# A two-layer decoder step on one core: norm parameters and p rows asked for during the last unit, the first weight half in two quarters

## The chip, the cores and the metric

The kernel runs on one core of one Trainium2 chip. The metric is the device time of one execution in microseconds (us). The engines are TensorE (PE, with PEld for its weight loads), VectorE (DVE), ScalarE (ACT), GpSimd (POOL) and SyncE (SP). SP issues most transfers through the hardware queue, GpSimd issues the others through the software queue, and all of them share 16 DMA engines.

## The reference

576 token rows of width 1024 (512 of a prompt, 64 of decode samples) pass through two layers. All arrays are float32.

```python
# layer 0: mixer A (chunked gMLP); layer 1: mixer B (short gated convolution)
x = layer_norm(DEEPNORM_ALPHA * x + mix, ln1_g[i], ln1_b[i])
moe = hier_moe(x, ...)      # 16 experts, two of them per token
x = layer_norm(DEEPNORM_ALPHA * x + moe, ln2_g[i], ln2_b[i])
gate = jax.nn.sigmoid(x @ ple_w_gate[i] + ple_b_gate[i])
x = x + gate * (p[i] @ ple_w_proj[i])
```

`layer_norm` is (x - mean) * rsqrt(var + 1e-5) * g + b over the 1024 columns. Mixer A begins with z = gelu(x @ w_in + b_in), whose second 3072 columns are v.

## The kernel before

Every float32 operand of a product is split into a high part `whi`, `xhi`, ... (ScalarE writes a rounded copy) and a low part `wlo`, `xlo`, ... (VectorE subtracts), and TensorE adds three products for one. A weight unit is 128x2048 numbers, 1 MB. SP loads it into one of the slots of `raw`, ScalarE's `hi` and VectorE's `lo` split it. Each engine's queue is written out by hand, in order, and the engines are joined by semaphores: where an instruction waits, all that follow it on its engine wait too.

**The start.** SP asks for row tile 0 of x, then for the first weight unit in two halves (semaphores `fh_ld` and `wld[0]`), then for four more row tiles and further units. TensorE turns row tile 0 (eight transposes), ScalarE writes the high part of the first half (L973) and then the two halves of `xhi` (L979), VectorE writes the low part of the first half (L1363) and then the two halves of `xlo` (L1371). TensorE's first product (L2106) needs all of these for its k. The first half holds the weights of k = 0 and 1; tile 1 of x is turned between k = 1 and k = 2.

**The end of mixer A.** The first 3072 columns are made in 12 units of seven products (Strassen's scheme; `q_done` counts products, QS = 7 per unit, US = 12 units). The products read `xhi`, `xlo` and the sums `xdh`, `xdl`. Products 0, 1 and 5 of a unit read `xhi`. After the last unit TensorE adds the last rows of the out projection, row tile by row tile (`out_rows`): for tiles 0 and 1 it turns the sum so far (L2268) and multiplies with `a_w_out` (L2277 to L2279). Then come `p_turns` (L2288, turns the rows of p), `h_turns(0)` (L2297, turns the normed rows of tile 0), and tile 2.

**The first norm of a layer.** VectorE takes the statistics of a row tile (L1602, L1604), ScalarE the root of the variance (L1104), VectorE subtracts the mean and multiplies with g (L1612), takes the reciprocal, and multiplies with it and adds b (L1617). g and b lie in the tile `ln_params` (`lnp`, 128x2048), in the place of `xhi`; the rows of p (`p_tok`) lie behind them in the place of `xhi` too. The result is alpha times the norm, for which GpSimd multiplies both g and b by alpha (L896). For layer 0, L1612 of row tile 0 also waits until the products of row tile 1 are done. GpSimd's queue at this place, in layer 0:

```python
pool.wait_ge(q_done, QS * US)              # L884: all products of the last unit
for n, g in enumerate((x_in["ln1_g"], x_in["ln1_b"])):
    pool.dma_start(lnp[:, n, :], ...)      # L887
pool.dma_start(p_tok[:, 0:4, :], ...)      # L888, and L889 for the sample rows
router_loads(0)                            # L859 to L862, four loads, layer 0 only
pool.wait_ge(ln_ld, 32 * (l + 1))
pool.tensor_scalar(lnp[:, :, :], lnp[:, :, :], ALPHA, None, ALU.mult).then_inc(ln_ok, 1)   # L896
```

In layer 1 the loads wait for the last products of the convolution's in projection instead (L885), and there are no router loads there. SP waits for all products of the last unit too (L640) and then reloads the other rows of the sum (`sum_reload`, L641), followed by expert weights (L668). VectorE's queue behind the norm of tiles 0 and 1 is: the split of the router weights (L1579 to L1582, layer 0), the low parts of p (L1636) and of the turned rows (L1640), the statistics of tile 2.

Behind the norm stand the router, a mixture of experts (16 steps, three weight units each), the second norm and the gate, and in layer 0 the convolution of layer 1.

Of the kernel before, what the change touches and what calls it, by code (L numbers as in the profile page):

```python
# [5 lines left out]
P = 128  # L6
# [79 lines left out]
def trunk(nc, x_in, outs):  # L86
# [60 lines left out]
    eps = new("eps", [P, 1])  # L147
# [174 lines left out]
    with ctx:  # L322
# [34 lines left out]
        xi_st, xb_ld = [sem("x_scaled_stored0"), sem("x_scaled_stored1")], sem("sum_reloaded")  # L357
# [228 lines left out]
        def _(sp):  # L586
# [24 lines left out]
            sp.dma_start(raw[:, 0, 0:UNIT // 2].rearrange("p (k c) -> p k c", c=512), first[:, 0:2, :]).then_inc(fh_ld, 16)  # L611
# [26 lines left out]
            def sum_reload():  # L638
                sp.wait_ge(xb_ld, 32)
                sp.wait_ge(q_done, QS * US)  # L640
                sp.dma_start(xcols(xT, PA, T), sum_dram[:, :, PA:T].rearrange("k p t -> p k t")).then_inc(xb_ld, 16)  # L641
# [118 lines left out]
        def _(pool):  # L760
# [15 lines left out]
            ch.link(pool.memset(eps[:, :], EPS))  # L776
# [102 lines left out]
            for l in range(DEPTH):  # L879

                if l == 0:
                    for n in range(4):
                        pool.wait_ge(acc_st[n], 32 * (AR - 1))
                    pool.wait_ge(q_done, QS * US)  # L884
                pool.wait_ge(mt_done, M_P[l] - KT)  # L885
                for n, g in enumerate((x_in["ln1_g"], x_in["ln1_b"])):
                    pool.dma_start(lnp[:, n, :], g[l:l + 1, :].to_broadcast([P, D])).then_inc(ln_ld, 16)  # L887
                pool.dma_start(p_tok[:, 0:4, :], x_in["p_prompt"][l, 0].rearrange("(i p) d -> p i d", p=P)).then_inc(p_ld, 16)  # L888
                pool.dma_start(p_tok[0:TS, 4, :], x_in["p_sample"][l].rearrange("b s d -> (b s) d")).then_inc(p_ld, 16)  # L889
                if l == 0:  # L890
                    router_loads(0)
# [4 lines left out]
                pool.tensor_scalar(lnp[:, :, :], lnp[:, :, :], ALPHA, None, ALU.mult).then_inc(ln_ok, 1)  # L896
# [66 lines left out]
        def _(act):  # L963
# [8 lines left out]
            act.wait_ge(fh_ld, 16)  # L972
            act.activation(whi[:, 0, 0:UNIT // 2], raw[:, 0, 0:UNIT // 2], ACT.Copy).then_inc(fh_ok, 1)  # L973
            for i in range(NT):
                act.wait_ge(tr_done, TR_IN + i + 1)
                for b in range(2):
                    src = ps[:, turned_bank(TR_IN + i) + b, :].rearrange("p (k t) -> p k t", t=P)[:, :, 0:tok(i)]
                    dst = xhi[:, 0:KT * T].rearrange("p (k t) -> p k t", t=T)[:, 4 * b:4 * b + 4, P * i:P * i + tok(i)]
                    act.activation(dst, src, ACT.Copy).then_inc(xhi_ok, 1)  # L979
# [120 lines left out]
            def std_tile(l, i):  # L1100

                t = tok(i)
                act.wait_ge(st_ok, NT * l + i + 1)
                act.activation(rstd[0:t, i:i + 1], mv[0:t, i, 1:2], ACT.Sqrt, bias=eps[0:t, 0:1]).then_inc(sq_ok, 1)  # L1104

            for l in range(DEPTH):
# [50 lines left out]
                act.activation(warm[:, :], eps[:, :], ACT.Exp)  # L1157
# [33 lines left out]
                def moe_step(s, it=0, step=0):  # L1191
# [4 lines left out]
                    if s == 0 and not step:  # L1196
                        act.activation(warm[:, :], eps[:, :], ACT.Silu)
# [87 lines left out]
                act.activation(warm[:, :], eps[:, :], ACT.Sqrt)  # L1285
# [67 lines left out]
        def _(dve):  # L1353
# [11 lines left out]
            half_lo(fh_ok, 0).then_inc(fh_ok, 1)  # L1365
            for i in range(NT):
                for b in range(2):
                    src = ps[:, turned_bank(TR_IN + i) + b, :].rearrange("p (k t) -> p k t", t=P)[:, :, 0:tok(i)]
# [224 lines left out]
            for l in range(DEPTH):  # L1593
# [12 lines left out]
                def norm_of(i):  # L1606
# [4 lines left out]
                    dve.wait_ge(ln_ok, l + 1)  # L1611
# [4 lines left out]
                    dve.wait_ge(rs_ok, 2 + n1 + i + 1)  # L1616
                    dve.scalar_tensor_tensor(out=xtok[0:t, i, :], in0=xtok[0:t, i, :], scalar=rstd[0:t, i:i + 1], in1=lnp[0:t, 1, :],  # L1617
# [425 lines left out]
        def _(pe):  # L2043
# [76 lines left out]
            for a in range(2):  # L2120
                for i in range(NT):
# [3 lines left out]
                    if i == 0 and a == 0:  # L2125
                        pe.wait_ge(fh_ok, 2)
                        v_half(0, a, i, range(0, 2))
# [129 lines left out]
            def out_rows(l, gl_n, d, pair_sem=None, pair_n=0):  # L2257
# [3 lines left out]
                def row_turns(i):  # L2261
                    if i >= 2:
                        pe.wait_ge(nz_ok, 2 * NT * l + i - 1)
                        if l == 0:
                            pe.wait_ge(xb_ld, 48)
# [104 lines left out]
                else:  # L2370
                    pe.wait_ge(xb_ld, 32)
# [363 lines left out]
```

## Time and profile before

| what | value |
|---|---|
| time, median of 3 runs | 1252.3 us (1251.42 to 1253.66) |
| profiled execution, its time | 1253.47 us |
| its span in the trace | 1251.4 us |
| TensorE busy | 1210.2 us, 97% |
| VectorE busy | 902.8 us, 72% |
| ScalarE busy | 618.6 us, 49% |
| GpSimd busy | 213.8 us, 17% |
| chain that ended last | TensorE 69%, DMA 13%, VectorE 9%, ScalarE 5%, issue 3%, GpSimd 1% |

The span runs from the first to the last instruction of the trace; the time of the same execution is 2.1 us longer. The chain that ended last is followed back from the last instruction, at each step to what released it. "Issue" is time in which an engine waited for nothing that the trace shows.

### The profile page before, as it was taken

What the parts mean: (1) busy time and instruction counts of PE and PEld (TensorE: products, weight loads), DVE (VectorE), ACT (ScalarE), POOL (GpSimd) and SP (SyncE); (2) the same over time, 40 slices, a digit from 0 to 9 for tenths busy, and PEclk for the clock granted to TensorE, in tenths of its full rate; (3) what the DMA queues carried; (4) which work ended last, traced back from release to release, by engine and by line L of the source; (5) the groups of instructions that cost most, each with busy time, mean ns of one, the idle gap of its engine ahead of it and who ended that gap; (6) DMA issues with size and microseconds to landing.
All of it is one profiled execution on the core that took longest, in us unless ns stands there. A gap on an engine that the chain in (4) does not pass through costs nothing.

```text
span 1251.4 us, 19263 instructions
## 1 busy us (share of the span) xinstructions
PE 1210.2 (97%) x7563; PEld 1094.5 (87%) x7563; DVE 902.8 (72%) x1238; ACT 618.6 (49%) x744; POOL 213.8 (17%) x246
## 2 busy tenths in 40 slices
PE   7999999999999998999999999999999999999898
PEld 6888889999999996888778699999998888878698
DVE  5554898687786876888889785445434889889793
ACT  5232444444344442488787574111211478878661
POOL 2311002131221312122431001000002022221100
PEclk9999999999999998999999999999999999999999
DMA  9456327594865954489998563322322369999522
GB/s 319 144 183 210 113 86 196 130 213 143 186 159 122 220 178 160 150 326 373 367 376 301 196 186 92 101 68 71 132 71 86 144 260 362 383 379 359 205 51 77
DMA packets 99583, 246.50 MB, mean 197 GB/s; under 512 B 10694, under 2 KB 55886, under 8 KB 87216
## 3 DMA queue, kind: packets, MB, share of 16 engines
q1 hardware_dynamic: 68976, 182.20, 41.4%
q0 software_dynamic: 30528, 63.20, 17.9%
q8 instruction: 55, 0.90, 0.3%
q14 instruction: 24, 0.20, 0.0%
HBM read 212.50 MB, written 49.62 MB: 209 GB/s over the span
## 4 chain that ended last, share of the span: by engine, by line
PE 69%; DMA 13%; DVE 9%; ACT 5%; issue 3%; POOL 1%; SPq 0%; DVEq 0%; POOLq 0%; ACTq 0%
PE ps L2055 13%; PE ps L2057 13%; PE ps L2056 13%; DMA w_raw<-in_moe_w_gate_up 7%; PE ps L2106 3%; PE ps L2108 3%; PE ps L2107 3%; PE ps L2471 2%; DVE w_lo L1359 2%; PE ps L2473 2%; PE ps L2472 2%; ACT w_hi L969 2%; DMA x_gathered<-y_scratch 1%; DMA ln_params<-in_ln_b 1%; PE ps L2163 1%
## 5 line engine op out<-in xcount | busy, mean ns | idle before, releaser
L1359 DVE TENSOR_TENSOR w_lo<-w_raw,w_hi 128x2048 fp32r<-128x2048 f32 (+1 forms) x133 | 290.2, 2191 | 66.6 <-ACT w_hi L969 58.0
L969 ACT ACTIVATE w_hi<-w_raw 128x2048 fp32r<-128x2048 f32 (+1 forms) x121 | 219.5, 1826 | 34.7 <-PE ps L2057 16.1
L2055 PE MATMUL ps<-x_hi,w_hi 128*128 128x288 f32 (+2 forms) x784 | 233.9, 298 | 1.9 <-DVE x_lo L1929 1.6
L2057 PE MATMUL ps<-x_hi,w_lo 128*128 128x288 f32 (+2 forms) x784 | 231.6, 295 | 0.0
L2056 PE MATMUL ps<-x_lo,w_hi 128*128 128x288 f32 (+2 forms) x784 | 231.6, 295 | 0.0
L2055 PEld LDWEIGHTS ps<-x_hi,w_hi 128*128 128x128 f32 x784 | 148.2, 189 | 3.6 <-issue 2.4
L2056 PEld LDWEIGHTS ps<-x_lo,w_hi 128*128 128x128 f32 x784 | 148.2, 189 | 0.0
L2057 PEld LDWEIGHTS ps<-x_hi,w_lo 128*128 128x128 f32 x784 | 148.2, 189 | 0.0
L2055 PE MATMUL ps<-g_hi,w_hi 128*128 128x288 f32 x384 | 114.6, 298 | 1.6 <-DVE g_lo L1495 0.7
L2057 PE MATMUL ps<-g_hi,w_lo 128*128 128x288 f32 x384 | 113.3, 295 | 0.0
L2056 PE MATMUL ps<-g_lo,w_hi 128*128 128x288 f32 x384 | 113.1, 294 | 0.0
L2471 PE MATMUL ps<-w_hi,xgT_hi 128*128 128x512 f32 x256 | 103.8, 406 | 6.3 <-DVE xgT_lo L1768 6.2
L2473 PE MATMUL ps<-w_hi,xgT_lo 128*128 128x512 f32 x256 | 100.9, 394 | 0.0
L2472 PE MATMUL ps<-w_lo,xgT_hi 128*128 128x512 f32 x256 | 100.2, 392 | 0.0
L1359 DVE TENSOR_TENSOR w_lo<-w_raw_more,w_hi 128x2048 fp32r<-128x2048 f32 x30 | 68.1, 2292 | 15.1 <-ACT w_hi L969 14.0
L2106 PE MATMUL ps<-w_hi,x_hi 128*128 128x512 f32 x192 | 75.8, 395 | 2.4 <-DVE x_lo L1371 2.4
L2055 PEld LDWEIGHTS ps<-g_hi,w_hi 128*128 128x128 f32 x384 | 72.1, 188 | 3.8 <-DVE g_lo L1495 1.6
L2108 PE MATMUL ps<-w_hi,x_lo 128*128 128x512 f32 x192 | 75.4, 392 | 0.0
L2107 PE MATMUL ps<-w_lo,x_hi 128*128 128x512 f32 x192 | 75.3, 392 | 0.0
L2056 PEld LDWEIGHTS ps<-g_lo,w_hi 128*128 128x128 f32 x384 | 72.1, 188 | 0.0
L2057 PEld LDWEIGHTS ps<-g_hi,w_lo 128*128 128x128 f32 x384 | 72.0, 188 | 0.0
L907 POOL DMA_INDIRECT x_gathered<-x_scratch,slot_token x32 | 41.2, 1288 | 152.7 <-PE ps L2437 123.6
(342 smaller groups left out, 2595.7 us busy)
## 6 DMA issues: line engine op xcount, KB each, us to landing
w_raw<-in_moe_w_gate_up SPq DMA_DIRECT2D x34, 1024.0 KB
w_raw<-in_moe_w_down SPq DMA_DIRECT2D x32, 1024.0 KB
w_raw_more<-in_moe_w_gate_up SPq DMA_DIRECT2D x30, 1024.0 KB
w_raw<-in_a_w_in SPq DMA_DIRECT2D x23, 1024.0 KB
w_raw<-in_a_w_out SPq DMA_DIRECT2D x12, 1024.0 KB
w_raw<-in_b_w_in SPq DMA_DIRECT2D x12, 1024.0 KB
sum_scratch<-out_stage POOLq DMA_DIRECT2D x40, 288.0 KB, 6.7
w_raw<-in_ple_w_gate SPq DMA_DIRECT2D x8, 1024.0 KB
```

The costliest lines, as they stand in the source:

```text
L907: pool.indirect_dma_start(out=xg[:, s % 2, :], out_offset=None, in_=x_dram[l][:, :], in_offset=bass.IndirectOffsetOnAxis(ap=idx[:, s:s + 1 ...
L969: act.activation(unit_of(whi, d), raw_unit(d), ACT.Copy).then_inc(hi_done, 1)
L1359: dve.tensor_tensor(unit_of(wlo, d), raw_unit(d), unit_of(whi, d).bitcast(f32), ALU.subtract).then_inc(split_done, 1)
L2055: pe.matmul(out, sh, mh, start=first, stop=False)
L2056: pe.matmul(out, sh, ml, start=False, stop=False)
L2057: ins = pe.matmul(out, sl, mh, start=False, stop=final)
L2106: pe.matmul(v_bank(i), xh_, wh, start=first, stop=False)
L2107: pe.matmul(v_bank(i), xh_, wl, start=False, stop=False)
L2108: ins = pe.matmul(v_bank(i), xl_, wh, start=False, stop=final)
L2471: pe.matmul(ps[:, 0, :], xs[0], ws[0], start=(a == 0 and k == 0), stop=False)
L2472: pe.matmul(ps[:, 0, :], xs[0], ws[1], start=False, stop=False)
L2473: ins = pe.matmul(ps[:, 0, :], xs[1], ws[0], start=False, stop=(a == 1 and k == 3))
```

## The change

The diff shows all edits but five in which `eps[:, :]` became `eps[:, 0:1]`.

```diff
     valid = new("valid", [P, NT])
-    eps = new("eps", [P, 1])
+    eps = new("eps", [P, 2])
     cols = new("cols", [P, NCOL])
...
         td_ok, tdh_ok, tdl_ok = sem("x_combined"), sem("x_combined_hi_ready"), sem("x_combined_lo_ready")
-        xi_st, xb_ld = [sem("x_scaled_stored0"), sem("x_scaled_stored1")], sem("sum_reloaded")
+        xi_st, xb_ld = [sem("x_scaled_stored0"), sem("x_scaled_stored1")], sem("part_loaded")
         acc_st = [sem(f"sum_added{n}") for n in range(4)]
...
             first = rows4(w_in, 0, AW)
-            sp.dma_start(raw[:, 0, 0:UNIT // 2].rearrange("p (k c) -> p k c", c=512), first[:, 0:2, :]).then_inc(fh_ld, 16)
+            for n, quarter_ld in enumerate((fh_ld, xb_ld)):
+                sp.dma_start(raw[:, 0, 512 * n:512 * n + 512], first[:, n, :]).then_inc(quarter_ld, 16)
             sp.dma_start(raw[:, 0, UNIT // 2:].rearrange("p (k c) -> p k c", c=512), first[:, 2:4, :]).then_inc(wld[0], 16)
...
             def sum_reload():
-                sp.wait_ge(xb_ld, 32)
+                sp.wait_ge(xb_ld, 48)
                 sp.wait_ge(q_done, QS * US)
...
             pool.memset(valid[:, :], 1.0)
-            ch.link(pool.memset(eps[:, :], EPS))
+            pool.memset(eps[:, 0:1], EPS)
+            ch.link(pool.memset(eps[:, 1:2], EPS / ALPHA ** 2))
             ch.link(pool.memset(wss[:, :, :], 0.0))
...
                         pool.wait_ge(acc_st[n], 32 * (AR - 1))
-                    pool.wait_ge(q_done, QS * US)
+                    pool.wait_ge(q_done, QS * (US - 1) + 1)
                 pool.wait_ge(mt_done, M_P[l] - KT)
...
                     pool.dma_start(lnp[:, n, :], g[l:l + 1, :].to_broadcast([P, D])).then_inc(ln_ld, 16)
+                if l == 0:
+                    pool.wait_ge(q_done, QS * US - 1)
                 pool.dma_start(p_tok[:, 0:4, :], x_in["p_prompt"][l, 0].rearrange("(i p) d -> p i d", p=P)).then_inc(p_ld, 16)
...
                 if l == 0:
+                    pool.wait_ge(q_done, QS * US)
                     router_loads(0)
...
                 pool.wait_ge(ln_ld, 32 * (l + 1))
-                pool.tensor_scalar(lnp[:, :, :], lnp[:, :, :], ALPHA, None, ALU.mult).then_inc(ln_ok, 1)
+                pool.tensor_scalar(lnp[:, 1, :], lnp[:, 1, :], ALPHA, None, ALU.mult).then_inc(ln_ok, 1)
                 for i in range(NT):
...
 
-            act.wait_ge(fh_ld, 16)
-            act.activation(whi[:, 0, 0:UNIT // 2], raw[:, 0, 0:UNIT // 2], ACT.Copy).then_inc(fh_ok, 1)
+            def quarter_hi(n):
+                act.wait_ge((fh_ld, xb_ld)[n], 16)
+                if n:
+                    act.wait_ge(fh_ok, 2)
+                act.activation(whi[:, 0, 512 * n:512 * n + 512], raw[:, 0, 512 * n:512 * n + 512], ACT.Copy).then_inc(fh_ok, 1)
+
+            quarter_hi(0)
             for i in range(NT):
...
                 for b in range(2):
+                    if i == 0 and b:
+                        quarter_hi(1)
                     src = ps[:, turned_bank(TR_IN + i) + b, :].rearrange("p (k t) -> p k t", t=P)[:, :, 0:tok(i)]
...
                 act.wait_ge(st_ok, NT * l + i + 1)
-                act.activation(rstd[0:t, i:i + 1], mv[0:t, i, 1:2], ACT.Sqrt, bias=eps[0:t, 0:1]).then_inc(sq_ok, 1)
+                act.activation(rstd[0:t, i:i + 1], mv[0:t, i, 1:2], ACT.Sqrt, bias=eps[0:t, 1:2], scale=1 / ALPHA ** 2).then_inc(sq_ok, 1)
 
...
 
-            half_lo(fh_ok, 0).then_inc(fh_ok, 1)
+            def quarter_lo(n):
+                dve.wait_ge(fh_ok, 1 + 2 * n)
+                c = slice(512 * n, 512 * n + 512)
+                dve.tensor_tensor(wlo[:, 0, c], raw[:, 0, c], whi[:, 0, c].bitcast(f32), ALU.subtract).then_inc(fh_ok, 1)
+
+            quarter_lo(0)
             for i in range(NT):
                 for b in range(2):
+                    if i == 0 and b:
+                        quarter_lo(1)
                     src = ps[:, turned_bank(TR_IN + i) + b, :].rearrange("p (k t) -> p k t", t=P)[:, :, 0:tok(i)]
...
                         dve.wait_ge(mt_done, rows_done(0, 1))
-                    dve.wait_ge(ln_ok, l + 1)
+                    dve.wait_ge(ln_ld, 32 * (l + 1))
                     dve.scalar_tensor_tensor(out=xtok[0:t, i, :], in0=ps[0:t, b:b + 2, :].rearrange("p b t -> p (b t)"), scalar=mv[0:t, i, 0:1],
...
                     dve.wait_ge(rs_ok, 2 + n1 + i + 1)
+                    dve.wait_ge(ln_ok, l + 1)
                     dve.scalar_tensor_tensor(out=xtok[0:t, i, :], in0=xtok[0:t, i, :], scalar=rstd[0:t, i:i + 1], in1=lnp[0:t, 1, :],
...
                     if i == 0 and a == 0:
-                        pe.wait_ge(fh_ok, 2)
-                        v_half(0, a, i, range(0, 2))
+                        for n in range(2):
+                            pe.wait_ge(fh_ok, 2 + 2 * n)
+                            v_half(0, a, i, range(n, n + 1))
                         input_turn(1)
...
                         if l == 0:
-                            pe.wait_ge(xb_ld, 48)
+                            pe.wait_ge(xb_ld, 64)
                     for k in range(KT):
...
                 else:
-                    pe.wait_ge(xb_ld, 32)
+                    pe.wait_ge(xb_ld, 48)
                     pe.wait_ge(c_done, CS * US - 2)
...
                     pe.wait_ge(c_done, CS * US)

```

The edits, in words:

- Start: the first half of the first weight unit is asked for as two transfers of 128x512 (`fh_ld` and `xb_ld`, so later waits on `xb_ld` count 16 more). ScalarE and VectorE split each quarter by itself; the second quarter's split stands between the two halves of tile 0 of x on both engines. TensorE waits for one quarter before k = 0 and for the other before k = 1.
- Layer 0: GpSimd asks for g and b once the first product of the last unit is done, for the rows of p once its sixth is done, for the router's arrays once all seven are done.
- Both layers: GpSimd multiplies only b by alpha. g stays as loaded: ScalarE takes the root of (var + eps) / alpha^2 instead, at the same place. VectorE's first pass waits for the loads, its second pass for GpSimd.

## Rows read from the trace of the kernel before

**Rows 1.** The chain that ended last, in order of time: start us, length us, what.
```profile
7.19 1.23 DVE w_lo L1363
...
461.57 11.30 DMA ln_params<-in_ln_b
...
472.96 5.40 POOL ln_params L896
...
478.48 1.28 DVE x_tok L1612
...
587.38 15.50 DMA w_raw<-in_moe_w_gate_up
...
946.69 5.97 DMA ln_params<-in_ln_b
...
952.75 5.40 POOL ln_params L896
```

**Rows 2.** Timeline of the start, all engines: start us, length us, engine line operation.
```profile
4.77 1.94 PE L2048 MATMUL ps<-ident,x_rows_in 128*128 128x128 f32 x8 [4.77 <-DMA x_rows_in<-in_x_prompt]
...
6.10 1.06 ACT L973 ACTIVATE w_hi<-w_raw 128x1024 fp32r<-128x1024 f32 x1 [4.01 <-DMA w_raw<-in_a_w_in]
...
7.06 1.06 ACT L979 ACTIVATE x_hi<-ps 128x512 fp32r<-128x512 f32 x2
...
8.33 1.28 DVE L1371 TENSOR_TENSOR x_lo<-ps,x_hi 128x512 fp32r<-128x512 f32 x2
...
9.07 0.80 PE L2106 MATMUL ps<-w_hi,x_hi 128*128 128x512 f32 x1 [2.36 <-DVE x_lo L1371]
```

**Rows 3.** Timeline of TensorE where layer 0's first norm begins.
```profile
473.94 0.40 PE L2279 MATMUL ps<-w_hi,g_lo 128*128 128x512 f32 x1
...
477.88 1.97 PE L2288 MATMUL ps<-ident,p_tok 128*128 128x128 f32 x8 [3.55 <-DMA p_tok<-in_p_sample]
...
481.56 1.97 PE L2297 MATMUL ps<-ident,x_tok 128*128 128x128 f32 x8 [1.71 <-DVE x_tok L1617]
```

**Rows 4.** Timeline of TensorE where layer 1's first norm begins.
```profile
958.34 1.03 PE L2288 MATMUL ps<-ident,p_tok 128*128 128x128 f32 x8
...
960.97 1.09 PE L2297 MATMUL ps<-ident,x_tok 128*128 128x128 f32 x8 [1.60 <-DVE x_tok L1617]
```

**Rows 5.** Timeline of VectorE, layer 0's first norm.
```profile
466.00 3.49 DVE L1359 TENSOR_TENSOR w_lo<-w_raw,w_hi 128x2048 fp32r<-128x2048 f32 x3
...
485.66 0.22 DVE L1579 MEMSET w_router_hi_lo<- 128x192 f32 x1
...
491.62 1.29 DVE L1602 BATCH_NORM_STATS2 v_stats<-ps 128x6 f32<-128x512 f32 x2 [2.89 <-PE ps L2279]
```

**Rows 6.** Timeline of VectorE, layer 1's first norm.
```profile
953.47 0.21 DVE L1604 BATCH_NORM_AGGREGATE mean_var<-v_stats 128x2 f32<-128x12 f32 x1
...
968.56 1.29 DVE L1602 BATCH_NORM_STATS2 v_stats<-ps 128x6 f32<-128x512 f32 x2 [1.16 <-PE ps L2279]
```

**Rows 7.** Stretches with TensorE's busy time: granted clock, share of DMA, GB/s.
```profile
449.00:460.00 11.00, 11.00 (x86) 1.00 0.01 1
...
477.00:486.50 9.50, 6.90 (x28) 0.50 0.38 148
...
958.40:962.80 4.40, 2.80 (x26) 1.00 0.10 41
```

**Rows 8.** Timeline of the issuing queues and of ScalarE around the last unit.
```profile
452.45 0.41 ACT L1061 ACTIVATE g_full<-ps 128x288 f32<-128x288 f32 x1 [0.95 <-DVE g_lo L1495]
...
460.39 0.36 SPq L641 DMA_DIRECT2D xT<-sum_scratch  x1
...
465.74 0.56 POOL L862 DMA_DIRECT2D b_router<-in_moe_b_expert  x1
...
509.88 0.33 SPq L668 DMA_DIRECT2D w_raw_more<-in_moe_w_gate_up  x1
```

**Rows 9.** Transfers of 440 to 480 us: size, microseconds from issue to landing.
```profile
b_router<-in_moe_b_expert POOLq DMA_DIRECT2D x1, 8.0 KB, 15.0
```

More of the change, by code:

```diff
@@ L1156, in _ @@
                 std_tile(l, 4)
-                act.activation(warm[:, :], eps[:, :], ACT.Exp)
+                act.activation(warm[:, :], eps[:, 0:1], ACT.Exp)
                 proj_out(1)
@@ L1196, in moe_step @@
                     if s == 0 and not step:
-                        act.activation(warm[:, :], eps[:, :], ACT.Silu)
+                        act.activation(warm[:, :], eps[:, 0:1], ACT.Silu)
                     q = it * step + (NE * l + s)
@@ L1283, in out_copy @@
                     act.activation(o_sb[0:tok(i), i, 512 * h:512 * h + 512], out_bank(u)[0:tok(i), :], ACT.Copy).then_inc(out_a, 1)
-                act.activation(warm[:, :], eps[:, :], ACT.Sqrt)
+                act.activation(warm[:, :], eps[:, 0:1], ACT.Sqrt)
                 squares(0)
```

## The prediction

> **What bounds the kernel now.** I read the page first: TensorE is busy for 97% of the span, and 69% of the chain that ended last is its work, so a change counts only where that chain leaves TensorE. Then I read the chain in order of time and looked for other engines' pieces. Three places belong to this change [rows 1]: the split of the first weight half at 7.19; in layer 0 a load of the norm's parameters of 11.30 us, followed by GpSimd's product of 5.40; in layer 1 the same pair with 5.97 and 5.40. The timelines of those places say what each waits for, the stretches say at which clock TensorE ran there, and the queues and landings say what the moved loads will meet. In layer 0 TensorE ends its products at 474.34 (473.94 + 0.40), idles 3.55 us for the rows of p, turns them, and idles 1.71 more for the first normed tile [rows 3]. In layer 1 it idles only 1.60, because its products last until 958.34 and the turns of p follow at once [rows 4].
>
> **The start.** Before, VectorE splits the whole first half (7.19 + 1.23 = 8.42) and only then takes x [rows 1, 2]: its first half of x is done near 8.97, and TensorE's first product comes 0.1 later, at 9.07. ScalarE began that half of x at 7.06 though the turned rows were there at 6.71 (4.77 + 1.94), since its weight copy ended only then [rows 2]. After: the half weight landed at 6.07, 1.3 us behind x; its first quarter has half the bytes and should land near 5.4. Its copy takes about 0.6 (a little over half of 1.06) and its subtraction about 0.68, so both end by 6.75. ScalarE takes x at 6.75 to 7.35, VectorE to 8.02 (halves of the pairs of 1.06 and 1.28), and the first product starts near 8.12: 0.95 earlier. The second quarter is copied by 7.95 and subtracted by 8.70; TensorE needs it after three products, which it begins 0.43 apart at this point, so after 9.4. The second weight half is split by about 10.8 and needed near 11.9. The extra issue delays the later x tiles by some 0.4 us on SP, which the two products' time covers. What can eat into 0.95 is the slow pace of the first products: if the pace doubles at the same moment as before and not with the work, half of the 0.95 is lost. Bounds 0.5 and 1.0; I take 0.8, nearer to the top, because each step has a row. From here to 452 the chain holds TensorE and its splits, so this is carried along.
>
> **Layer 0, loads.** The first product of the last unit is done by 452.45, when ScalarE takes it; all seven are done by 460.39, when SP's reload goes out [rows 8]. Between 449 and 460 the DMA engines are 1% busy [rows 7]. So g and b, asked for at 452.5 and 453.1, should land as in layer 1, 5.97 us behind the second issue [rows 1], or near 459; even with the 11.30 of before they are there by 465. The condition for the rows of p falls one product before the end, about (460.39 - 452.45) / 6 = 1.3 earlier, at 459.1, and their second issue at 459.9. Before, they landed at 477.88 with 1 MB of parameters ahead of them, some 15 us behind their issue. If they still took 15 us they would be there at 474.9, and their turns (1.03 at full clock [rows 4]) would be over at 476, before the normed tile. I expect them near 470, under the products. The router's last load was issued at 465.74 and landed 15.0 later, at 480.7 [rows 8, 9]; VectorE takes it at 485.66 [rows 5]. Four issues are gone from ahead of it (some 2.3 us), so with the same delay it lands at 478.4, and VectorE will ask at 481.6: hidden by 3. GpSimd waits at this place with nothing behind it but these issues and the scaling.
>
> **Layer 0, the norm.** GpSimd's product has half the elements: 2.7 us of the 5.40 [rows 1]. It runs behind the router's issues, near 464 to 466.7, long before VectorE's second pass. VectorE's first pass then waits only for the products of row tile 1, which end at 474.34. Before, TensorE's turns came 3.08 us behind the start of that pass (481.56 - 478.48) [rows 1, 3]. So they start at 474.43 + 3.08 = 477.5 and not at 481.56: **4.05 us**. The turns of p lie in the gap before.
>
> **Layer 0, the clock.** From 477.0 to 486.5 TensorE ran at a granted clock of 0.50, its lower level of 1.2 GHz, after it had idled 3.55 us [rows 7, 3]. In layer 1 the same turns, with an idle time of 1.60 between them, ran at 1.00, the 2.4 GHz level [rows 7, 4]. From the turns of tile 0 to the statistics of tile 2 layer 0 takes 491.62 - 481.56 = 10.06 and layer 1 takes 968.56 - 960.97 = 7.59 [rows 3 to 6]. Afterwards TensorE idles in layer 0 from about 475.4 to 477.5, 2.1 us, which is nearer to the 1.60 than to the 3.55. I take it that the clock holds: **2.45 us** more. VectorE has time for this: it idles 1.16 in layer 1 before those statistics [rows 6], and the split of the router weights, four short operations from 485.66 on, is the only work that layer 0 has beyond that [rows 5]. Together 6.5 us. The Trainium skill, "TensorE: Matmul & The Clock Gate", section on PE-mode transpose, says that turns don't engage the full clock as products do. By that rule the clock would fall here, for nothing but turns runs from 474.3 to 479.3, and the sum would be 6.45 in place of 8.9. The trace speaks against it in layer 1, where 4.4 us of turns and idle time kept 1.00 [rows 7].
>
> **Layer 1.** The loads are not moved. They land at 952.75 [rows 1]; VectorE has its statistics at 953.68 [rows 6] and can start its first pass there, while GpSimd scales b until 955.45. The second pass ends near 956.8, before 958.34 + 1.03 = 959.37, when the turns of p are through. The wait ends there and TensorE is the bound: 960.97 - 959.37 = **1.60 us** [rows 4]. A slower scaling would still be hidden by 2.5 us. ScalarE's root with a scale is the same instruction; the second memset is a tenth of a microsecond on GpSimd, at the start, before anyone asks for it.
>
> **What carries it to the end.** The next expert loads are issued at 509.88, when the row products are through [rows 8], so they move with the chain, and so does the stream of weights whose 15.50 us the chain contains at 587.38 [rows 1].
>
> **The sum.** 0.8 + 6.5 + 1.6 = 8.9 us off the profiled execution's 1253.5 (span 1251.4 and 2.1 around it): 1244.6. The median of the runs is 1.2 below that execution, so I forecast 1252.3 - 8.9 = 1243.4 us.
>
> **The rivals.**
> - *The clock falls all the same in layer 0* and the stretch takes its 10.06 us: the gain is 0.8 + 4.05 + 1.6 = 6.45, time 1245.9. For it: 2.1 us of idle time with only turns on both sides has no row. Against it: layer 1 with 1.60. Chance 0.20.
> - *GpSimd's scaling collides with VectorE.* Before, it stood beside statistics; now it stands at 464 to 466.7, beside a low part of g and the first of the three `w_lo` at 466.00 [rows 5], which read two arrays in SBUF. That `w_lo` ends near 468.3 and TensorE needs it 0.3 later. If the two engines took turns for the 1.4 us of overlap, TensorE would lose 1.1: time 1244.5. No row shows such an overlap. The Trainium skill, "GPSIMD Engine Reference", section on specifications, says that the two contend when VectorE has two SBUF inputs. Chance 0.10.
> - *The stream of expert weights absorbs it.* If the stretch around 587 were bound by transfers whose pace is not tied to the row stage, all before it would be lost and 1.6 remain: 1250.7. Against it: the issue at 509.88. Chance 0.05.
> - *The loads don't come earlier where it matters*: the rows of p wait behind the reload of x and the expert weights until 477.9 as before. The turns of p then run at the lower clock to 479.85, the gain in layer 0 is 1.7, and the time 1252.3 - 4.1 = 1248.2; where g and b are late too, there is no gain in layer 0 and it is 1249.9. Chance 0.07.
> - *Slower: the clock falls at 475.4 and stays down.* Before, it was down for some 10 us. Each microsecond of work at 1.2 GHz costs half of one. With the 8.9 gained, the time passes that of before once 18 us are spent there; if it lasted until the router is through at 530, it would cost 25 and give 1268. Nothing in the profile shows so long a fall. Chance 0.03.
>
> **How the numbers follow.** The forecast keeps 0.55. Its own range is 1242.3 to 1244.7: the terms at 9.1 and 8.6 and about 1 us between runs. The stated range, 1241.5 to 1247.0, takes in the first two rivals and leaves out 0.15. A measurement of this kernel can tell about 0.2%, 2.5 us, from no change. Below 1249.8 lie the forecast, the first two rivals and the first part of the fourth: 0.90. Within 0.2%: the stream, and the late g and b, 0.07. Slower: 0.03.
>
> **What would show it.** First product near 8.1. `ln_params` issued at about 452 and landed by 459, L896 2.7 us long before 467. TensorE goes from its products into the turns of p without waiting, idles about 2 us, turns tile 0 about 3.1 us behind the products' end, at a clock of 1.00, and the statistics of tile 2 follow 7.6 later. In layer 1 no idle time before L2297. The prediction is wrong if the clock row reads 0.50 there, if `w_lo` at 466 is longer than 2.3, or if a new DMA wait stands on TensorE before 530.

## The result and the profile after

| what | before | after |
|---|---|---|
| time, median of 6 runs each on one chip | 1252.05 us (1251.01 to 1253.66) | 1245.21 us (1242.97 to 1247.69) |
| profiled execution, its time | 1253.47 us | 1246.35 us |
| its span | 1251.4 us | 1243.9 us |
| ratio after / before, 95% interval | | 0.9944 [0.9929, 0.9959] |

The change makes the kernel 6.8 us faster, where 8.9 were forecast; the time lies within the stated range. The six executions of the changed kernel fall into two groups of three: 1242.97, 1243.89 and 1244.08, which is near the forecast 1243.4, and 1246.35, 1246.41 and 1247.69. The median, 1245.21, lies between the groups, where no execution was. TensorE's mean granted clock is on record for each execution: 1.000 for all three of the first group, 0.999, 0.998 and 0.999 for the second. The profiled execution (0.999) belongs to the second group, so its trace can say what is missing. One execution of an experiment below (e1) took 3053.67 us and is left out of its ratio.

**The start.** Timeline of all engines in the changed kernel, which answers [rows 2] (L1380 splits a quarter, L2126 to L2128 are the products, L2068 turns x):

```profile
5.89 0.69 DVE L1380 TENSOR_TENSOR w_lo<-w_raw,w_hi 128x512 fp32r<-128x512 f32 x1 [5.89 <-ACT w_hi L981]
6.69 0.60 ACT L991 ACTIVATE x_hi<-ps 128x512 fp32r<-128x512 f32 x1 [0.82 <-PE ps L2068]
...
8.06 0.79 PE L2126 MATMUL ps<-w_hi,x_hi 128*128 128x512 f32 x1 [1.41 <-DVE x_lo L1390]
...
10.79 1.91 PE L2068 MATMUL ps<-ident,x_rows_in 128*128 128x128 f32 x8
...
12.92 0.63 PE L2127 MATMUL ps<-w_lo,x_hi 128*128 128x512 f32 x1
...
13.35 0.55 PE L2128 MATMUL ps<-w_hi,x_lo 128*128 128x512 f32 x1
...
13.74 0.40 PE L2126 MATMUL ps<-w_hi,x_hi 128*128 128x512 f32 x1
```

The same stretch of TensorE before the change:

```profile
11.79 1.32 PE L2048 MATMUL ps<-ident,x_rows_in 128*128 128x128 f32 x8
12.87 0.47 PE L2106 MATMUL ps<-w_hi,x_hi 128*128 128x512 f32 x1
...
13.64 0.40 PE L2106 MATMUL ps<-w_hi,x_hi 128*128 128x512 f32 x1
```

The first product starts at 8.06, 1.01 us earlier than at 9.07 [rows 2], each step as forecast. But products that take 0.63 us (slow pace) turn into products that take 0.40 (full pace) at 13.4 to 13.7 in the changed kernel; before, the pace had doubled by 12.9. The eight turns between k = 1 and k = 2 take 1.91 us where they took 1.32. At the first product of k = 3 (13.74 against 13.64) nothing is left of the 1.01 in this pair of traces. The granted clock is shown as 1.00 in these stretches in both kernels. But the record behind that column has its first entry only at 13.7 us in the changed kernel's trace and at 12.4 in the one before (an estimate, counted back from the falls near 477), which is where the pace doubles; the slow pace ahead of it is seen in the durations alone.

**Layer 0.** TensorE in the changed kernel, the answer to [rows 3] (L2309 turns p, L2318 the normed tile 0, L2289 the sum of tile 2):

```profile
474.52 0.39 PE L2300 MATMUL ps<-w_hi,g_lo 128*128 128x512 f32 x1
474.75 1.03 PE L2309 MATMUL ps<-ident,p_tok 128*128 128x128 f32 x8
477.73 1.87 PE L2318 MATMUL ps<-ident,x_tok 128*128 128x128 f32 x8 [1.95 <-DVE x_tok L1637]
479.39 1.91 PE L2289 MATMUL ps<-ident,xT 128*128 128x128 f32 x8
```

VectorE and GpSimd there, the answer to [rows 5] and [rows 8]:

```profile
465.90 0.76 DVE L1514 TENSOR_TENSOR g_lo<-g_full,g_hi 128x576 fp32r<-128x576 f32 x1 [0.76 <-ACT g_hi L1060]
466.58 3.49 DVE L1371 TENSOR_TENSOR w_lo<-w_raw,w_hi 128x2048 fp32r<-128x2048 f32 x3
...
475.00 1.28 DVE L1631 SCALAR_TENSOR_TENSOR x_tok<-ps,mean_var,ln_params 128x1024 f32<-128x1024 f32 x1 [1.24 <-PE ps L2300]
...
476.39 1.28 DVE L1637 SCALAR_TENSOR_TENSOR x_tok<-x_tok,rstd,ln_params 128x1024 f32<-128x1024 f32 x1
...
486.98 1.29 DVE L1621 BATCH_NORM_STATS2 v_stats<-ps 128x6 f32<-128x512 f32 x2 [2.08 <-PE ps L2300]
```

```profile
451.48 0.54 POOL L889 DMA_DIRECT2D ln_params<-in_ln_b  x1
459.60 0.76 POOL L892 DMA_DIRECT2D p_tok<-in_p_prompt  x1 [7.58 <-PE ps L2077]
...
464.49 2.83 POOL L901 TENSOR_SCALAR ln_params<-ln_params 128x1024 f32<-128x1024 f32 x1
```

The stretches, the answer to [rows 7] (us, TensorE busy, granted clock, share of DMA, GB/s):

```profile
474.90:477.70 2.80, 0.88 (x9) 1.00 0.47 196
478.00:481.00 3.00, 3.00 (x17) 0.50 0.43 172
482.00:486.50 4.50, 4.50 (x21) 1.00 0.28 117
```

VectorE's first pass waits for the products alone (1.24 us, released by TensorE), and the turns of p follow the products at once. From the end of the products to the turns of tile 0 it is 477.73 - 474.91 = 2.82 us, where it was 481.56 - 474.34 = 7.22 [rows 3]: 4.40 gained. At 478 the granted clock falls to 0.50, the 1.2 GHz level, and is back at 1.00 (2.4 GHz) by 482. From the turns of tile 0 to the statistics of tile 2 it takes 486.98 - 477.73 = 9.25 us, against 10.06 before and 7.59 in layer 1: 0.81 of the forecast 2.45 is gained.

**Layer 1.** TensorE in the changed kernel, the answer to [rows 4], and VectorE, the answer to [rows 6]:

```profile
953.35 1.03 PE L2309 MATMUL ps<-ident,p_tok 128*128 128x128 f32 x8
954.22 1.04 PE L2318 MATMUL ps<-ident,x_tok 128*128 128x128 f32 x8
```

```profile
950.58 1.28 DVE L1637 SCALAR_TENSOR_TENSOR x_tok<-x_tok,rstd,ln_params 128x1024 f32<-128x1024 f32 x1 [0.49 <-POOL ln_params L901]
...
961.75 1.30 DVE L1621 BATCH_NORM_STATS2 v_stats<-ps 128x6 f32<-128x512 f32 x2 [1.62 <-PE ps L2300]
```

No idle time is left. From the turns of p to the statistics of tile 2 it takes 8.40 us where it took 968.56 - 958.34 = 10.22: 1.82 gained.

So the two traces differ by 4.40 + 0.81 + 1.82 = 7.0 us in the norms. The times of the two executions differ by 7.1 and their spans by 7.5; what differs elsewhere nearly cancels. At the end of layer 0's products the changed kernel's trace is 0.57 us behind (474.91 against 474.34), 0.1 of it from the start and some 0.4 from a late piece of ScalarE and VectorE near 294 us. Before, TensorE had another slow stretch in layer 1's experts, which the changed kernel's trace hasn't; it is worth about 1.7 us (an estimate: half of the 3.4 us that it lasted, since at 0.53 the same work takes about twice the time):

```profile
1107.90:1111.50 3.60, 3.60 (x11) 0.53 0.83 330
```

Most of that was lost again: from the statistics of tile 2 in layer 1 to TensorE's last turns (which start at 1235.82 before and at 1228.81 after) the lead grows by 0.2 us only. Why wasn't followed.

### The profile page after: what moved, and what is told of

Its sections match the earlier page's. It is cut to its first block, busy times and chain, and to the rows that moved or that the text cites. A ratio compares the mean times of both kernels' runs of the same rounds, so it can differ in the third digit from the quotient of the medians.

```text
span 1243.9 us, 19268 instructions
## 1 busy us (share of the span) xinstructions
PE 1208.4 (97%) x7563; PEld 1093.4 (88%) x7563; DVE 903.1 (73%) x1239; ACT 618.2 (50%) x745; POOL 210.1 (17%) x247
## 4 chain that ended last, share of the span: by engine, by line
PE 72%; DMA 12%; DVE 9%; ACT 4%; issue 3%; SPq 0%; DVEq 0%; POOLq 0%; ACTq 0%
PE ps L2075 13%; PE ps L2077 13%; PE ps L2076 13%; DMA w_raw<-in_moe_w_gate_up 8%; PE ps L2126 3%; PE ps L2127 3%; PE ps L2128 3%; DVE w_lo L1371 2%; PE ps L2492 2%; PE ps L2494 2%; PE ps L2493 2%; ACT w_hi L974 2%; PE ps L2298 2%; PE ps L2300 1%; PE ps L2299 1%
## 5 line engine op out<-in xcount | busy, mean ns | idle before, releaser
L2126 PE MATMUL ps<-w_hi,x_hi 128*128 128x512 f32 x192 | 76.1, 396 | 1.4 <-DVE x_lo L1390 1.4
L2128 PE MATMUL ps<-w_hi,x_lo 128*128 128x512 f32 x192 | 75.5, 393 | 0.0
```

The source lines that it names most:

```text
L2126: pe.matmul(v_bank(i), xh_, wh, start=first, stop=False)
L2128: ins = pe.matmul(v_bank(i), xl_, wh, start=False, stop=final)
```

## The experiments

The times below are medians and ratios to the kernel before, on the same chip in the same set of executions.

### Which part carries the gain: e1 and e2

e1 is the kernel before with the start's edits alone, e2 the changed kernel without them.

```diff
-            sp.dma_start(raw[:, 0, 0:UNIT // 2].rearrange("p (k c) -> p k c", c=512), first[:, 0:2, :]).then_inc(fh_ld, 16)
+            for n, quarter_ld in enumerate((fh_ld, xb_ld)):
+                sp.dma_start(raw[:, 0, 512 * n:512 * n + 512], first[:, n, :]).then_inc(quarter_ld, 16)
```

> Only the start of the change: the first weight half in two quarters; the norm as before. Theory A (the first product comes 1.0 us earlier, but TensorE reaches its full pace at a moment that isn't tied to it): first product at 8.1 against 9.07, and at 40 us anything between 1.0 earlier and level; median time 0 to 1 us under the kernel before. Rival (the gain is carried whole, what was lost in the changed kernel came from the norm's part): 1.0 us under. Rival (the extra transfer delays the later tiles of x): a new wait for x rows before 25 us, time over that of before.

> Only the norm's part of the change; the first weight half as before. Theory A: 6 to 8.5 us under the kernel before, within 1 us of the changed kernel, since the start gives little. Rival (the start gives its 1.0): 1.0 us over the changed kernel. In both, executions lie in two groups some 2 to 3 us apart, by whether TensorE's clock falls behind the gap in layer 0.

Measured: e1 1252.03 us, ratio 0.9994 [0.9984, 1.0003]; e2 1246.45, ratio 0.9945 [0.9932, 0.9959]. The start's part is worth 0.8 us by its ratio, with no gain at all inside its interval, and the rest alone gives the changed kernel's ratio (0.9944). Everything that is clear of the noise comes from the norm's part. In e1's trace the first product starts at 8.02 and TensorE is at full pace by 12.3; in the changed kernel's it was 13.7. How much of the 1 us survives differs from execution to execution, so one pair of traces can't price it. All traces together can, roughly. The first product of k = 3 starts at 13.48 to 14.67, on average 13.90, in the six traces with the first half in one piece (before, e2, e3, e4, e7, e8), and at 12.72 to 13.74, on average 13.06, in the four with quarters and no extra turns at the start (the changed kernel, e1, e5, e6): 0.84 us earlier. At the split of a weight unit near 455 us, the same averages are 455.72 and 455.24, 0.48 us apart, with ranges that overlap.

### The loads and the scaling, each alone: e3 and e4

e3 is the kernel before with the early loads alone (g and b both scaled, as before). e4 is the kernel before with the halved scaling alone (the loads at their old time).

```diff
 e3
-                    pool.wait_ge(q_done, QS * US)
+                    pool.wait_ge(q_done, QS * (US - 1) + 1)
...
+                if l == 0:
+                    pool.wait_ge(q_done, QS * US - 1)
                 pool.dma_start(p_tok[:, 0:4, :], ...)
...
                 if l == 0:
+                    pool.wait_ge(q_done, QS * US)
                     router_loads(0)
 e4
-                pool.tensor_scalar(lnp[:, :, :], lnp[:, :, :], ALPHA, None, ALU.mult).then_inc(ln_ok, 1)
+                pool.tensor_scalar(lnp[:, 1, :], lnp[:, 1, :], ALPHA, None, ALU.mult).then_inc(ln_ok, 1)
...
-                    dve.wait_ge(ln_ok, l + 1)
+                    dve.wait_ge(ln_ld, 32 * (l + 1))
...
+                    dve.wait_ge(ln_ok, l + 1)
```

> Only the earlier loads of layer 0; g and b are both scaled by GpSimd as before. Theory (in layer 0 the loads are what counts, since the scaling of 5.4 us now lies under the products; in layer 1 the scaling is what counts): layer 0 as in the changed kernel, turns of tile 0 about 2.9 us behind the end of the products; layer 1 unchanged, with TensorE idle 1.6 us; 1.7 us over the norm-only kernel, about 4.5 to 6.5 under the kernel before. Rival (GpSimd's scaling beside VectorE's splits costs): the low part of the weights at 466 takes over 2.3 us and TensorE waits for it.

> Only the scaling of b alone, with the loads asked for when they were before. Theory: in layer 0 the rows of p now end the wait: they land near 477.9 as before, their turns follow, and the turns of tile 0 directly behind them at 479.9, 1.7 us earlier than before, at the lower clock; layer 1 gains 1.7; 3.4 us under the kernel before. Rival (the parameters end the wait, p is by the way): layer 0 gains 4, as in the changed kernel.

Measured: e3 1250.01 us, ratio 0.9983 [0.9974, 0.9992]; e4 1245.87, ratio 0.9956 [0.9942, 0.9969]. Both expectations failed. e3 brings 2.1 us where 4.5 to 6.5 were expected, and its rival came true in part: not the low part of the weights but one of g is longer, and TensorE waits for it (next section). For e4, 3.4 us were expected, and half the scaling alone brings 5.5 us of the changed kernel's 7.0 by the ratios; the two intervals overlap. (Each ratio's distance from 1, times 1252.)

Timeline of e4, GpSimd, VectorE and TensorE:

```profile
462.85 0.57 POOL L890 DMA_DIRECT2D p_tok<-in_p_sample  x1
...
472.15 2.79 POOL L897 TENSOR_SCALAR ln_params<-ln_params 128x1024 f32<-128x1024 f32 x1 [5.84 <-DMA ln_params<-in_ln_b]
```

```profile
474.44 1.28 DVE L1613 SCALAR_TENSOR_TENSOR x_tok<-ps,mean_var,ln_params 128x1024 f32<-128x1024 f32 x1 [1.25 <-PE ps L2281]
...
476.17 1.28 DVE L1619 SCALAR_TENSOR_TENSOR x_tok<-x_tok,rstd,ln_params 128x1024 f32<-128x1024 f32 x1 [0.37 <-DVE rstd L1616]
```

```profile
476.93 1.09 PE L2290 MATMUL ps<-ident,p_tok 128*128 128x128 f32 x8 [2.58 <-DMA p_tok<-in_p_sample]
477.86 1.04 PE L2299 MATMUL ps<-ident,x_tok 128*128 128x128 f32 x8
```

With the loads at their old time, g and b have landed by 472.1, 2.3 us before the products end. What had kept VectorE's first pass until 478.48 [rows 1] was the scaling of g behind the landing, not the landing. Now that pass reads g as loaded and waits for the products alone (1.25 us), and GpSimd scales b before the second pass asks for it. The rows of p land at 476.9. Their turns then fill the time in which VectorE finishes tile 0, and the turns of tile 0 follow without a wait at 477.86, 3.5 us behind the products, against 2.82 in the changed kernel. In this trace the clock held, so the statistics of tile 2 come 7.54 us behind those turns (485.40 - 477.86), against 9.25.

### GpSimd and VectorE side by side: e3, e7, e8

e7 is e3 with the scaling in two instructions of 128x1024. e8 is e3 with the scaling held back until ScalarE and VectorE have split the last part of g.

```diff
 e7
-                pool.tensor_scalar(lnp[:, :, :], lnp[:, :, :], ALPHA, None, ALU.mult).then_inc(ln_ok, 1)
+                pool.tensor_scalar(lnp[:, 0, :], lnp[:, 0, :], ALPHA, None, ALU.mult)
+                pool.tensor_scalar(lnp[:, 1, :], lnp[:, 1, :], ALPHA, None, ALU.mult).then_inc(ln_ok, 1)
 e8
+                if l == 0:
+                    pool.wait_ge(gl_done, ROUND * AR)
                 pool.tensor_scalar(lnp[:, :, :], lnp[:, :, :], ALPHA, None, ALU.mult).then_inc(ln_ok, 1)
```

> The loads-only kernel (loads of layer 0 early, g and b both scaled), with GpSimd's scaling of 128x2048 written as two instructions of 128x1024. In the loads-only kernel one low part of g on VectorE took 2.90 us in place of 0.76 while GpSimd scaled. If the long single instruction is what holds VectorE up: 0.76 again, 2 us under the loads-only kernel (1248). If it is any work of GpSimd at this moment: as the loads-only kernel, 1250.

> The loads-only kernel, with GpSimd's scaling of 128x2048 held back until VectorE's last low part of g is done (near 466); it then stands beside the three low parts of weights. If GpSimd and VectorE get in each other's way whenever VectorE reads two arrays in SBUF: one of the low parts of weights is longer by up to 2 us, TensorE waits, 1250 or more. If not: every low part as long as before, 1248.

Measured: e7 1249.63 us, ratio 0.9977 [0.9968, 0.9987]; e8 1248.01, ratio 0.9962 [0.9950, 0.9973]. Timelines of GpSimd and VectorE, first e3, then e7, then e8:

```profile
463.86 5.43 POOL L899 TENSOR_SCALAR ln_params<-ln_params 128x2048 f32<-128x2048 f32 x1
...
465.27 2.90 DVE L1498 TENSOR_TENSOR g_lo<-g_full,g_hi 128x576 fp32r<-128x576 f32 x1 [0.75 <-ACT g_hi L1051]
468.10 3.48 DVE L1362 TENSOR_TENSOR w_lo<-w_raw,w_hi 128x2048 fp32r<-128x2048 f32 x3
```

```profile
464.04 2.83 POOL L899 TENSOR_SCALAR ln_params<-ln_params 128x1024 f32<-128x1024 f32 x1
466.82 2.78 POOL L900 TENSOR_SCALAR ln_params<-ln_params 128x1024 f32<-128x1024 f32 x1
...
465.46 0.76 DVE L1499 TENSOR_TENSOR g_lo<-g_full,g_hi 128x576 fp32r<-128x576 f32 x1 [0.76 <-ACT g_hi L1052]
466.13 5.10 DVE L1363 TENSOR_TENSOR w_lo<-w_raw,w_hi 128x2048 fp32r<-128x2048 f32 x3
```

```profile
467.41 7.26 POOL L901 TENSOR_SCALAR ln_params<-ln_params 128x2048 f32<-128x2048 f32 x1 [2.38 <-DVE g_lo L1500]
...
467.14 6.94 DVE L1364 TENSOR_TENSOR w_lo<-w_raw,w_hi 128x2048 fp32r<-128x2048 f32 x3
```

e7's first half of the scaling leaves `g_lo` at 0.76, but the time is that of the second case, any work of GpSimd. In e8 the low parts are longer, as in its first case, but the time is that of the second, 1248. The 5.40 us scaling beside VectorE's subtractions costs time, in another place each time: in e3 one `g_lo` takes 2.90 us in place of 0.76, in e7 the three `w_lo` take 5.10 in place of 3.49 [rows 5], in e8 they take 6.94 and the scaling itself 7.26. TensorE feels it most in e3, where `g_lo` is awaited:

```profile
468.23 0.50 PE L2280 MATMUL ps<-w_hi,g_hi 128*128 128x512 f32 x1 [0.92 <-DVE g_lo L1498]
```

In the changed kernel the scaling of b alone, beside the same `g_lo` and the first 0.7 us of `w_lo`, costs nothing: 0.76 and 3.49, as before. So halving it does two things: it ends the wait, and it makes the early place harmless. Why 2.83 us of GpSimd's work there isn't felt and 5.4 us is, in two instructions as in one, stays open.

e8 shows something else too. It scales g and b in full and gains nothing in layer 1 (TensorE idles 1.39 us there), yet its ratio is worth 4.8 us, where e3's is worth 2.1. So the early loads can end layer 0's wait without the halving, if the scaling stays clear of the `g_lo` that TensorE waits for. In its trace the turns of tile 0 start 3.2 us behind the products (478.65 - 475.47), where it was 7.22. The two edits are two ways to about the same gain in layer 0.

### The clock in layer 0's gap: e5 and e6

Both are the changed kernel with work for TensorE between the turns of p and those of tile 0 in layer 0, in banks that nothing reads before they are written again. The results aren't used.

```diff
                 p_turns(0)
                 p_turns(1)
+                if l == 0:
+                    gap_work(n)
                 h_turns(0)
 e5: 8 products of 128x512 of constants, some 2.1 us
 e6: 17 turns of 128x128 of constants, some 2.0 us
```

> The changed kernel, with eight extra products of ones (128x512, result unused) on TensorE in layer 0's gap between the turns of p and the turns of tile 0, where it idles 1.95 us. Theory B (the gap is what makes the clock fall in some executions): the clock stays at the 2.4 GHz level, 7.6 us from the turns of tile 0 to the statistics of tile 2 in place of 9.25, the time is near 1243 in all executions, about 2 us under the changed kernel's median. Rival (the clock falls for another reason, or not there in most executions): no change in median or spread.

> The changed kernel, with 17 extra turns (transposes of a tile of ones, result unused) in the same gap in place of products. If turns hold the clock as products do: as with the products, near 1243 in all executions. If turns don't count for it: a stretch of 5 us of nothing but turns, the clock falls in most executions, and the time is 1246 or more.

Measured: e5 1244.46 us (1243.03 to 1246.21), ratio 0.9935 [0.9921, 0.9949]; e6 1243.43 (1242.62 to 1244.56), ratio 0.9922 [0.9909, 0.9936]. Timeline of TensorE and stretches in e6:

```profile
473.96 1.03 PE L2309 MATMUL ps<-ident,p_tok 128*128 128x128 f32 x8
474.83 2.02 PE L2376 MATMUL ps<-ident,ones 128*128 128x128 f32 x17
...
476.94 1.09 PE L2318 MATMUL ps<-ident,x_tok 128*128 128x128 f32 x8
```

```profile
474.80:478.90 4.10, 4.00 (x36) 1.00 0.31 124
```

From 474.0 to 478.9 TensorE does nothing but turns, and the clock stays at 1.00. The statistics of tile 2 stand at 484.53, 7.59 behind the turns of tile 0: the forecast's number. By the ratios (0.9935 and 0.9922 against 0.9944, times 1252) work in the gap brings 1.1 and 2.8 us; the intervals overlap with the changed kernel's, so neither is clear of the noise by itself. e6 shows no execution above 1244.6, e5 has two, 1245.40 and 1246.21, so "near 1243 in all executions" failed for e5. The three executions of e5 with a mean granted clock of 1.000 (1243.03, 1243.91, 1244.46) and the three of e6 (1242.62, 1243.43, 1244.56) are as fast as the three of the changed kernel with 1.000. That the gap's idle time makes the clock fall is therefore likely, since both traces with work in it held the clock there, but not proved: e9's and e4's traces hold it too without such work, and falls come elsewhere as well (e6's trace has one near 1130 us, in layer 1's experts). The Trainium skill, "TensorE: Matmul & The Clock Gate", section on PE-mode transpose, has it that transposes don't engage the full clock; by the row above, and by e9 below, it doesn't hold here. A fall such as it would give did come in the changed kernel's profiled execution, but not from the turns: with more of them in the gap the clock held.

### The start: e9 and e10

e9 is the changed kernel with 13 turns of constants before x has landed and 6 behind the turns of tile 0; e10 adds e6's turns in the gap. None of their results is used.

```diff
+            pe.wait_ge(ident_ok, 1)
+            start_turns(13)
             pe.wait_ge(ident_ok, 2)
...
             input_turn(0)
+            start_turns(6)
```

> The changed kernel, with 13 extra turns of a tile of ones on TensorE before x arrives and 6 more behind the turns of row tile 0 (results unused). Theory A (TensorE's pace doubles after it has worked for a while, and turns count as work): the pace doubles before 10 us in place of 13.7, the products of the start run at 0.23 us apart earlier, 2 to 3 us under the changed kernel. Rival (turns don't count): the doubling stays at 12 to 14 us, same time.

> The changed kernel with both fillings of turns, at the start and in layer 0's gap: the sum of both, near 1241, and the least spread between executions.

Measured: e9 1243.34 us, ratio 0.9927 [0.9914, 0.9940]; e10 1241.81 (1241.12 to 1243.77), ratio 0.9915 [0.9902, 0.9928]. e9 is 2.1 us under the changed kernel by the ratios, as theory A has it, but the intervals overlap; e10 is 3.6 us under it, and its interval lies just below the changed kernel's. Timeline of TensorE in e9:

```profile
1.74 2.98 PE L2098 MATMUL ps<-ident,ones 128*128 128x128 f32 x13 [1.74 <-POOL ident L766]
4.68 1.07 PE L2068 MATMUL ps<-ident,x_rows_in 128*128 128x128 f32 x8
5.58 0.82 PE L2098 MATMUL ps<-ident,ones 128*128 128x128 f32 x6
7.22 0.50 PE L2133 MATMUL ps<-w_hi,x_hi 128*128 128x512 f32 x1 [0.81 <-DVE x_lo L1390]
...
7.79 0.40 PE L2135 MATMUL ps<-w_hi,x_lo 128*128 128x512 f32 x1
9.20 0.50 PE L2133 MATMUL ps<-w_hi,x_hi 128*128 128x512 f32 x1 [1.02 <-DVE w_lo L1380]
```

The turns of constants alone bring TensorE to full pace: those of x take 1.07 us where they took 1.94, and the first products take 0.40, not 0.63. (In e12's trace it comes later: the turns of x still take 1.91 us, the first products 0.40.) With that the earlier work is kept: TensorE has the third product of k = 2 at 12.00, where the changed kernel has it at 13.35. A new wait of 1.02 us stands before k = 1, for the second quarter's low part, which the slow pace had hidden. The clock in the gap stayed at 1.00 in e9's trace without any filling.

### The early loads with the clock held: e11 and e12

e12 is e10's kernel once more. e11 is the same with the loads at their old time, and with the 17 turns ahead of those of p.

```diff
-                    pool.wait_ge(q_done, QS * (US - 1) + 1)
+                    pool.wait_ge(q_done, QS * US)
...
+                if l == 0:
+                    gap_work(17)
                 p_turns(0)
                 p_turns(1)
-                if l == 0:
-                    gap_work(17)
```

> This is the version with turns at the start and in layer 0's gap, with the loads put back to where they were before the change: GpSimd asks for g, b, the rows of p and the router's arrays only when all products of the last unit are done. The 17 turns of the gap stand ahead of the turns of p here. Only b is scaled. It tells what the early loads bring when the clock is held in both. Theory A (halving the scaling carried layer 0's gain and the early loads add nothing that can be measured): the rows of p land near 477, the turns of tile 0 follow near 478, and the time is within 0.7 us of that of the version with early loads, 1241.8: 1241.8 to 1242.5. Theory B (the loads bring something that the loss of clock in the gap hid): the turns of p come about 2 us later, the rest of the norm behind them too, and the time is 1.5 to 2 us above it, near 1243.5. If the router's arrays land so late that VectorE waits for them, there is a DMA wait at about 485 to 487 and the time is higher again.

> The version with turns at the start and in the gap and with the early loads once more, so that it and the one with the loads put back are compared on the same chip. Theory A: the two are within 0.7 us of each other. Theory B: this one is 1.5 to 2 us faster. By its earlier runs it takes 1241.8 us.

Measured: e11 1242.97 us, ratio 0.9935 [0.9921, 0.9949]; e12 1242.93, ratio 0.9926 [0.9913, 0.9939]. The medians differ by 0.04 us, which is theory A. The ratios differ by more, 1.1 us in favour of the early loads, because one execution of e11 took 1247.23 us; their intervals overlap, and theory B's lower end isn't excluded by them. The traces show what the early loads bring here: the statistics of tile 2 in layer 0 come 11.1 us behind the first turns after the products in e11 (484.13 - 473.04) and 10.6 in e12 (483.73 - 473.16), 0.5 us. Timeline of TensorE in e11:

```profile
473.04 2.02 PE L2380 MATMUL ps<-ident,ones 128*128 128x128 f32 x17
475.67 1.09 PE L2313 MATMUL ps<-ident,p_tok 128*128 128x128 f32 x8 [0.61 <-DMA p_tok<-in_p_sample]
476.60 1.04 PE L2322 MATMUL ps<-ident,x_tok 128*128 128x128 f32 x8
```

The last rows of p landed 13.9 us behind their issue (15.0 before the change, 14.0 in e4, 4.3 in the changed kernel), and that was in time for all but half a microsecond. The best version of all runs is e10, with 1241.8 and 1242.9 us in its two sets.

## Why the prediction was right, and where it was not

- **The start, 0.8 us: right up to the first product, not settled behind it.** Each step up to the first product came as worked out: 1.01 us for a forecast of 0.95. How much is kept behind it is what the bounds 0.5 and 1.0 are about. The pair of traces, changed kernel and before, shows nothing kept, since the pace doubled over 1 us later in the changed kernel's trace. By e1's ratio it is 0.8 us with an interval that holds 0, by the averages over ten traces 0.84 at 14 us and 0.48 at 455. So the runs don't contradict the forecast term, and aren't sharp enough to confirm it. With TensorE brought to full pace first (e9), more is kept.
- **Layer 0, the loads: they came early, and were not needed once g is left as loaded.** g and b were asked for at 451, the rows of p at 459.6 and 460.4; the latter landed 4.6 and 4.3 us behind their issues in place of 11.8 and 15.0. The forecast had credited the loads and the halved scaling together with 4.05 us; it was 4.40. e4 and e11 show that the halved scaling alone carries nearly all of it: the traces give the early loads 0.5 to 0.7 us on top. e8 shows that early loads with a late scaling would have done as well. The rival that put 1248.2 on rows of p that land at 477.9 had its condition nearly met in e4 (476.9), and was wrong about its price: the turns of p then stand in the time that VectorE needs for tile 0 anyway.
- **Layer 0, the clock, 2.45 us: right as a mechanism, kept only in part of the executions.** The step "2.1 us, which is nearer to the 1.60 than to the 3.55" held in some executions and not in others. The gap was 1.95 us, and the clock fell in the profiled execution, though not for some 10 us as the rival had it: 0.81 came of 2.45. A fall as long as this one, from about 477.9 to 481.3, takes 0.0014 off an execution's mean granted clock (an estimate from the windows above). The three executions at 1243.0 to 1244.1, where the forecast put them, read 1.000, so they had no such fall anywhere; the others read less. That the single median comes out 1.8 us above the forecast is likely a matter of how many executions had one.
- **Layer 1, 1.60 us: right.** 1.82, with no wait left.
- **The rivals.** *The clock falls all the same* lies nearest to the median (1245.9 against 1245.21), and it is what happened in the profiled execution. *GpSimd's scaling collides*: not in the changed kernel, but with the full scaling it does (e3, e7, e8), which is the reason why the loads alone bring so little. Its text said that no row shows such an overlap. The Trainium skill, "GPSIMD Engine Reference", section on specifications, has the contention, and e3, e7 and e8 agree with it while the changed kernel's 0.76 and 3.49 do not. *The stream absorbs it* and *slower* are excluded by the result.

## What to carry to other kernels

When two edits in a change remove the same wait, price each alone: here the landing was in time already, and the product behind it was the wait. Moving an instruction of GpSimd to an early place can cost more than it saves if VectorE has work there that TensorE waits for (e3 against e8). Where TensorE idles for 2 to 3 us between stretches of turns, don't count on its clock. In the gap of layer 0, extra work without a use moved nothing (the turns of tile 0 start 2.98 us behind those of p in e6 and in the changed kernel), and the clock held there in every trace with it (e5, e6, e10 to e12). What an earlier start is worth depends on the moment at which TensorE's pace doubles, which differs between executions by more than the 1 us gained: judge it by several traces, not by one pair.

## What the runs showed that was not expected

- The length of the idle time alone doesn't decide the fall. With 1.95 us idle behind the turns of p the clock fell in the changed kernel's trace and held in e9's; with 2.58 us ahead of them it held in e4's.
- The falls are of different length: from about 477 to 486.5 at 0.50 before the change [rows 7], from 478 to about 481.5 after it. What ends them is open.
- TensorE's full pace at the start began between 11.5 and 14.5 us in the traces without turns of constants, and between about 4.5 and 7 with them.
- GpSimd's scaling and VectorE's subtractions beside each other: 2.83 us of GpSimd's work, the last 0.7 beside `w_lo`, unfelt; 5.4 us felt with 1.6 to 3.5 us on VectorE.
